# Last merge block finished by token thirds on VectorE, first output weights split one stage early, and constant products on TensorE ahead of the last stage

## What is computed

```
x = layer_norm(x_in)
z = x @ w_in + b_in                              # all projections and the merge gates
o_nsa, o_ml, o_fox = three token mixers of z     # 256 wide each
mix = (sum_b sigmoid(gate_b) * (o_b @ w_branch[b])) @ w_out
x1 = layer_norm(alpha * x + mix)
out = layer_norm(alpha * x1 + moe(x1))           # 16 experts, top group, then top 2 in it
```

## Time and profile before

| | us |
|---|---|
| three runs | 1513.5, 1512.06, 1507.91 |
| median of them | 1512.06 |
| profiled execution, its own time | 1509.91 |
| its span | 1508.3 |
| TensorE busy in it | 1368.0 (91%) |
| TensorE idle before the first product of mix (last product of merge to L2331) | 8.30 |
| TensorE idle before the last stage | 12.18 |

### The profile page before, as it was taken

One profiled execution on the slowest core, in us unless ns is written; L12 is line 12 of the kernel. 1 busy time (PEld: TensorE's weight loads), 2 busy tenths in 40 slices (PEclk: granted clock), 3 DMA queues, 4 the chain that ended last, 5 costly groups with the idle time before them and its releaser, 6 DMA issues. The chain is left out here.

```text
span 1508.3 us, 23664 instructions
## 1 busy us (share of the span) xinstructions
PE 1368.0 (91%) x8917; PEld 1185.3 (79%) x8917; DVE 611.7 (41%) x1593; ACT 516.6 (34%) x962; POOL 368.3 (24%) x463
## 2 busy tenths in 40 slices
PE   5999999999999999978888978979985999999965
PEld 3999999999888989956665657968865888888832
DVE  6222212222423324034667557863563233333317
ACT  5422222222122221126545656530001333434336
POOL 5211150020202000002333214621133322322307
PEclk9999999999999999969999999989995999999978
DMA  7244393162624224872004018762117787888954
GB/s 211 71 156 147 122 245 117 58 180 72 188 58 152 78 69 69 186 213 40 1 2 161 16 40 265 233 213 84 63 35 189 237 286 250 265 280 273 326 220 181
DMA packets 188963, 228.29 MB, mean 151 GB/s; under 512 B 47607, under 2 KB 157303, under 8 KB 187487
## 3 DMA queue, kind: packets, MB, share of 16 engines
q1 hardware_dynamic: 176270, 186.25, 41.1%
q0 software_dynamic: 12592, 40.71, 8.7%
HBM read 167.89 MB, written 60.19 MB: 151 GB/s over the span
## 5 line engine op out<-in xcount | busy, mean ns | idle before, releaser
L1255 PE MATMUL psum<-proj_x_hi,proj_w_hi 128*128 128x362 f32 (+1 forms) x1056 | 357.4, 338 | 3.4 <-DVE proj_w_lo L1380 2.2
L1255 PE MATMUL psum<-proj_x_hi,proj_w_lo 128*128 128x362 f32 (+1 forms) x1056 | 346.9, 329 | 0.0
L1255 PE MATMUL psum<-proj_x_lo,proj_w_hi 128*128 128x362 f32 (+1 forms) x1056 | 346.8, 328 | 0.0
L1255 PEld LDWEIGHTS psum<-proj_x_hi,proj_w_hi 128*128 128x128 f32 x1056 | 199.6, 189 | 10.4 <-POOL proj_x_lo L1461 2.5
L1255 PEld LDWEIGHTS psum<-proj_x_lo,proj_w_hi 128*128 128x128 f32 x1056 | 199.9, 189 | 0.0
L1255 PEld LDWEIGHTS psum<-proj_x_hi,proj_w_lo 128*128 128x128 f32 x1056 | 199.3, 189 | 0.0
L1380 DVE TENSOR_TENSOR proj_w_lo<-proj_w_raw,proj_w_hi 128x1024 fp32r<-128x1024 f32 x44 | 54.4, 1237 | 273.8 <-ACT proj_w_hi L1288 273.7
L1317 ACT ACTIVATE proj_sig<-psum,proj_bias 128x362 f32<-128x362 f32 (+1 forms) x72 | 40.4, 564 | 240.6 <-PE psum L1255 228.0
L2809 PEld LDWEIGHTS psum<-moe_xgt,expert_gate_w 128*128 128x128 f32 x512 | 85.2, 194 | 13.2 <-issue 13.2
L2809 PE MATMUL psum<-moe_xgt,expert_gate_w 128*128 128x192 f32 x512 | 92.1, 334 | 0.7 <-ACT moe_xgt L2854 0.7
L2809 PE MATMUL psum<-moe_xgt,expert_up_w 128*128 128x192 f32 x512 | 88.4, 326 | 0.0
(11 more groups left out here) (479 smaller groups left out, 2406.6 us busy)
## 6 DMA issues: line engine op xcount, KB each, us to landing
proj_w_raw<-in_w_in SPq DMA_DIRECT2D x43, 512.0 KB, 5.1
expert_gate_w<-in_moe_w_gate SPq DMA_DIRECT2D x16, 1024.0 KB, 5.6
expert_up_w<-in_moe_w_up SPq DMA_DIRECT2D x16, 1024.0 KB, 11.1
expert_down_w<-in_moe_w_down SPq DMA_DIRECT2D x16, 1024.0 KB, 8.0
merge_sig<-gate_scratch SPq DMA_DIRECT2D x24, 544.0 KB, 4.1
gate_scratch<-proj_sig SPq DMA_DIRECT2D x48, 181.0 KB, 2.0
feature_scratch<-proj_feat SPq DMA_DIRECT2D x13, 512.0 KB, 3.0
token_scratch<-proj_tok SPq DMA_DIRECT2D x10, 512.0 KB, 5.2
```

The lines of the kernel that those rows point to most:

```text
L1255: mm = nc.tensor.matmul(k.ps[u % RING][:, 0:w], b[wt][:, x % 2, kk, :], b[xx][:, kk, a0:a0 + w], start=(kk == 0 and i == 0), stop=(kk == K ...
```

## The change

1. In the last group of merge (g = 23) VectorE does the three adds itself, right after each third's multiplication, and POOL does none there. ScalarE makes `y_hi` of the last block in three copies, each after its third's add, and VectorE `y_lo` in three subtractions.
2. Piece 0 of `w_out` is split in merge: ScalarE's copy to `w0_hi` after its last sigmoid, VectorE's subtraction to `w0_lo` as the last of its list. Mix reads these for kk = 0 and splits only pieces 1 to 7; SP fetches piece 4 at once and pieces 5 to 7 after `w_lo` of pieces 1 to 3.
3. `XRES` falls from 4 to 2, so merge fetches two residual tiles, and mix fetches seven (two slots) where it fetched five.
4. After the experts TensorE multiplies the identity by 512 columns of constants 11 times into a PSUM bank that is not read (`keep_busy`), ahead of the last stage.

```diff
+def keep_busy(k, bank, n):
+    for _ in range(n):
+        k.nc.tensor.matmul(k.ps[bank][:, :], k.c("ident"), k.const[:, 0:512], start=True, stop=True)
...
-XRES = 4
+XRES = 2
...
+    pre |= {n: stack.enter_context(nc.sbuf_tensor(f"pre_{n}", [P, D], F32R)) for n in ("w0_hi", "w0_lo")}
...
@@ merge, scalar
-            high(KD - 1)
+                if g == UNITS - 1:
+                    act.wait_ge(ps["wo_loaded0"], 16)
+                    nc.scalar.copy(pre["w0_hi"][:, :], pre["w_raw"][:, 0, :]).then_inc(s["w0_hi_done"], 1)
+            for n, (a0, w) in enumerate(MCH):
+                act.wait_ge(s["ended"], n + 1)
+                nc.scalar.copy(y["hi"][:, KD - 1, a0:a0 + w], b["whole"][:, (KD - 1) % 2, a0:a0 + w]).then_inc(s["y_hi_done"], 1)
@@ merge, vector
-            low(KD - 1)
+                if g == UNITS - 1:
+                    dve.wait_ge(s["gated"], u + 1)
+                    dve.wait_ge(s["summed"], 6 * (KD - 1) + n + 1)
+                    nc.vector.tensor_tensor(dst, dst, b["part"][:, x % PARTS_AHEAD, 0:w], ALU.add).then_inc(s["ended"], 1)
+            for n, (a0, w) in enumerate(MCH):
+                dve.wait_ge(s["y_hi_done"], KD + n)
+                nc.vector.tensor_tensor(y["lo"][:, KD - 1, a0:a0 + w], b["whole"][:, (KD - 1) % 2, a0:a0 + w], y["hi"][:, KD - 1, a0:a0 + w].bitcast(F32), ALU.subtract).then_inc(s["y_lo_done"], 1)
+            dve.wait_ge(s["w0_hi_done"], 1)
+            nc.vector.tensor_tensor(pre["w0_lo"][:, :], pre["w_raw"][:, 0, :], pre["w0_hi"][:, :].bitcast(F32), ALU.subtract).then_inc(s["w0_lo_done"], 1)
@@ merge, gpsimd
-                if m:
+                if m and g < UNITS - 1:
@@ mix, sync
-                sp.wait_ge(s["w_lo_done"], kk - WRAW + 1)
+                if kk > WRAW:
+                    sp.wait_ge(s["w_lo_done"], kk - WRAW)
@@ mix, tensor
-                    if t == 0:
-                        pe.wait_ge(s["w_lo_done"], kk + 1)
+                    if t == 0 and kk >= 1:
+                        pe.wait_ge(s["w_lo_done"], kk)
...
+                            ws = b[ww][:, kk, :] if kk else pre["w0" + ww[1:]]
@@ mix, vector and scalar: the two loops that split the pieces
-            for kk in range(KD):
+            for kk in range(1, KD):
@@ experts, tensor
             all_rounds(pe, one_round)
+            keep_busy(k, 7, 11)
             last_tensor(pe)
```

More of the change, by code:

```diff
@@ L2063, in merge_branches @@
     st, b, s = phase(k, "merge", dict(sig=[P, SIGS, T], br_raw=[P, 3, 2, 364], br_hi=[P, 6, T], br_lo=[P, 6, T], branch_w=[P, RING, 2, P], branch_w_hi=[P, 2, 2, P], branch_w_lo=[P, 2, 2, P], part=[P, PARTS_AHEAD, 364], whole=[P, 2, T]),
-                     ["br_hi_done", "br_lo_done", "bw_hi_done", "bw_lo_done", "proj_mm", "sig_done", "gated", "summed", "y_hi_done", "y_lo_done"] + [f"br_loaded{m}_{n}" for m in range(3) for n in range(3)] + [f"sig_loaded{i}" for i in range(SIGS)] + [f"bw_loaded{i}" for i in range(RING)])
+                     ["br_hi_done", "br_lo_done", "bw_hi_done", "bw_lo_done", "proj_mm", "sig_done", "gated", "summed", "y_hi_done", "y_lo_done", "w0_hi_done", "w0_lo_done", "ended"] + [f"br_loaded{m}_{n}" for m in range(3) for n in range(3)] + [f"sig_loaded{i}" for i in range(SIGS)] + [f"bw_loaded{i}" for i in range(RING)])
     N = UNITS * 3
@@ L2281, in mix @@
                         for i, (yy, ww) in enumerate((("hi", "w_hi"), ("lo", "w_hi"), ("hi", "w_lo"))):
-                            mm = nc.tensor.matmul(k.ps[2 * (t % 2) + half][0:r, :], y[yy][:, kk, t * P:t * P + r], b[ww][:, kk, half * 512:(half + 1) * 512],
+                            ws = b[ww][:, kk, :] if kk else pre["w0" + ww[1:]]
+                            mm = nc.tensor.matmul(k.ps[2 * (t % 2) + half][0:r, :], y[yy][:, kk, t * P:t * P + r], ws[:, half * 512:(half + 1) * 512],
                                                   start=(kk == 0 and i == 0), stop=(kk == KD - 1 and i == 2))
@@ L2357, in low @@
             def low(kk):
-                dve.wait_ge(s["w_hi_done"], kk + 1)
+                dve.wait_ge(s["w_hi_done"], kk)
                 nc.vector.tensor_tensor(b["w_lo"][:, kk, :], pre["w_raw"][:, kk % WRAW, :], b["w_hi"][:, kk, :].bitcast(F32), ALU.subtract).then_inc(s["w_lo_done"], 1)
```

## The result

| | before | after |
|---|---|---|
| median of the runs of this comparison, us | 1506.72 (14) | 1500.4 (14) |
| lowest and highest run | 1501.55, 1513.5 | 1497.1, 1506.59 |
| ratio, 95% interval | | 0.9965 [0.9949, 0.9981] |
| span of the profiled execution | 1508.3 | 1501.0 |

The change makes the kernel faster by 0.35%, about 5.3 us (0.0035 x 1506.72). A second comparison gave 0.9971 [0.9953, 0.9989], 4.4 us. The forecast's shift, 4.6, lies between the two; its absolute time, 1506.4, is too high, and 1500.4 lies under the range's low end of 1501.5. Both have to be explained: the level, and what the right-looking sum is made of.

The account below looks back on a forecast made before the run. TensorE was taken to set the pace, with merge's end hanging on SP. Terms 3.5 + 0 + 0 + 1.1 = 4.6 us off a base of 1511.0 gave 1506.4, range 1501.5 to 1511.5.

Parts of the forecast that it names:

- the last of the sum: Whole kernel: the 4.6 us shift taken from a base of 1511.0, the middle of four known times, giving 1506.4.
- SP without two residual fetches: End of merge: SP ends 1.36 to 2.5 us earlier, middle 1.9, so mix's first instruction comes at 996.6.
- Rival (a): End of merge: VectorE or something else not SP holds the block; gain 2.7 at the least, 1508.3; chance 0.16.
- Adds on VectorE: Last group of merge: VectorE ends at 995.4 instead of 996.0, worth nothing by itself since SP ended later.
- The feared slowing of POOL: Last group of merge: POOL's adds meet VectorE's, third add 1.2 us later, VectorE ending at 996.6 as upper end.
- Piece 0 split ahead: Start of mix: the 1.56 us wait for the low part of the first weight piece goes wholly.
- merge to mix: From merge's last product to mix's first real one: that product comes at 997.4 instead of 1000.86, 3.5 us earlier.
- The clock at the start of mix: Start of mix: the clock falls again after a 6.4 us gap; no difference taken, -1.25 and +0.5 kept for the range.
- Two slots: Residual fetches in mix: tile t + 2 fetched in place of t + 4, 13.2 us of cover, cost nothing.
- rival (d): Residual add in mix, tiles 2 to 8: fetches are exposed and the kernel is slower, 1518.6; chance 0.03.
- Constant products: Before the last stage: eleven take 9.5 us, 2.7 stay idle, one low clock stretch; likeliest gain 1.1, ends 2.8 and -0.3.
- Rival (b): Gap before the last stage: no fall of the clock, total gain 6.3 us, 1504.7; chance 0.14.

Follow-up runs that it names:

- experiment 8: The unaltered changed kernel run twice more; 0.9971 beside the kernel before in one comparison, spans of its three traces 1501.0, 1495.5 and 1506.1.
- filler_only: The kernel before with only the eleven constant products added; ratio 0.998 [0.9963, 0.9997].
- six_pieces: The kernel before with VectorE's last y_lo of merge cut into six subtractions; one run, 1510.25 us.
- early_split_res_later: The changed kernel with piece 0 split at g = 21 and the residual tiles fetched in mix behind the pieces of w_out; ratio 0.9958 [0.9943, 0.9974].
- Experiments 2, 3, 5 and 6: In this order: two_slots_only; no_thirds; fetches_later and a sequel that also splits piece 0 at g = 21 (ratio 0.9954); early_split_res_later.
- experiment 4: The changed kernel with piece 0 of w_out split in mix as before; ratio 0.9971 [0.9957, 0.9985], merge to mix 7.72.
- two_slots_only: The kernel before with only XRES changed from 4 to 2; ratio 0.9989 [0.9974, 1.0004], merge to mix 8.45.
- no_thirds: The changed kernel with POOL's adds and whole y_hi and y_lo for the last block; ratio 0.9981 [0.9965, 0.9998], merge to mix 7.42.
- fetches_later: The changed kernel with seven small transfers moved from SP's merge list into mix, behind the pieces of w_out; ratio 0.9972 [0.9958, 0.9986].

## Why the prediction missed

**The level.** The step that failed is the last of the sum: "the four times known (with 1507.91 and 1513.5) have their middle at 1511.0, and from there it is 1506.4". The three runs shown (1507.91 to 1513.5) were high ones; the fourteen of the comparison have their median at 1506.72, 4.3 lower, and the four later groups of before lie at 1506.9 to 1508.5. With 1506.72 as the base the same shift of 4.6 gives 1502.1, inside the range; the remaining 1.7 is a shift of 6.3 by these two medians against the 4.6. The text counted 2 for the spread of medians, which was too little for a base of four executions: the fourteen runs of before spread over 12 (1501.55 to 1513.5), and experiment 8 shows traces of a single kernel 10.6 apart.

**SP without two residual fetches: undersized, by less than the first pair of traces says.** Forecast 1.9 (1.36 to 2.5). In the first pair SP came 3.63 earlier: 1.80 from issues where 1.36 stood, 1.50 from the standing of the two small fetches where about 0.5 was reckoned, and 0.27 from merge itself. Counted from merge's last product, SP ended after 7.62, 7.12 and 6.71 in the three traces with nothing of this part (before, filler_only, six_pieces), 7.15 in the mean, and after 4.26 to 5.01 in the eight traces with all of it, 4.75 in the mean. So the gain is 2.4, inside the stated 1.36 to 2.5.

The reason given, "3.96 for a fetch of four numbers per partition is no cost of its own: the queue was full", holds for a part only. The two small fetches (second router weights, first bias) stood together for 8.7 behind four residual tiles (three traces), 7.2 to 7.8 behind two (eleven traces), and still for 6.0 to 6.7 in the four kernels that had no residual tile just ahead of them. SP in early_split_res_later:

```profile
979.49 2.89 SPq L2103 DMA_DIRECT2D pre_w_r<-in_moe_w_expert  x1
982.42 3.47 SPq L2104 DMA_DIRECT2D pre_bias_r<-in_moe_b_group  x1
```

How much of these six is their own and how much comes from other transfers on the way is not separated by any run.

The reading that the block hung on SP was right for the kernel before (TensorE 0.68 after it). For the changed kernel SP at 995.9 and VectorE at 995.4 were forecast; they ended at 994.22 and 994.96 in the first trace, and level within 0.2 in the other seven. Not reckoned was that VectorE's end reaches TensorE sooner (0.32) than SP's (0.69), which keeps SP the holder in those seven. Rival (a), the block held by VectorE, came true in one trace of eight, by 0.37, and without its price: VectorE ended 1.6 before the feared 996.6. Experiments 2, 3, 5 and 6 show that VectorE is next as soon as SP's list is shortened or VectorE's lengthened.

**Adds on VectorE, "by itself this is worth nothing, since SP ended later": right by the rule, but needed in the sum.** The thirds were not run alone. With SP out of the way the arithmetic's end counts, and without the thirds the distance is 7.42. The feared slowing of POOL did not come: its first three adds of the block took 3.75, and the first three of the block ahead of it took 3.73 in the kernel before and 3.74 in the changed one, where nothing was moved; they ended at 990.06, before the forecast's 992. Of VectorE's adds only the first, which overlaps POOL's last, was a little longer (0.61 against 0.54).

**Piece 0 split ahead: right, a little undersized.** Forecast 1.56, experiment 4 shows 1.8. After the constants began, the real product came 0.42 later, not 0.77, so this way is 1.91 shorter (2.33 before). Waits for later pieces appear in three of the eight traces, 0.17 to 0.47 in all.

Together: merge to mix was forecast at 7.2 (997.4 - 990.23). Eight traces with the whole of this part have 5.74 to 6.12, mean 5.90; three without any of it 10.63, 10.14, 9.73, mean 10.17. The gain is 4.3 (2.4 and 1.9), forecast 3.5.

**The clock at the start of mix: near.** From the first product to the first residual add it is 13.64 in the mean of the same eight traces and 14.14 in that of the three: 0.5 gained where 0 was forecast, within what was kept open (from 1.25 gained to 0.5 lost).

**Two slots: right.** VectorE never waited for a residual fetch in mix; rival (d) had no part.

**Constant products: the mechanism right, the inference on the clock too firm.** 9.71 for 9.5, idle 2.34 for 2.7. "But 2.7 of idleness stay, and a gap of 1.97 was followed by a fall" rested on one gap of one trace. Over all traces the clock fell after that same 1.97 in 9 of 16, and after 2.3 to 2.6 behind eleven products in 3 of 11; after 5.00, 7.58 and 12 in 6 of 6. One low stretch after a short gap cost 1.1 to 1.7, about as forecast (1.7). So the first tile takes 3.96 in the mean of eleven traces with the products and 5.75 in the mean of four without (6.25, 5.30, 5.15, 6.31): they are worth 1.8, forecast 1.1. Rival (b) had too little chance at 0.14. The Trainium skill (TensorE: Matmul & The Clock Gate, Part 1) says that the monitor is free-running and that the slow matmuls at a kernel's start change in number from run to run of one kernel. The three traces of experiment 8 agree, at two places inside the kernel. The prediction quoted this rule for mix and did not apply it to the last gap or to the base.

**Not foreseen: 1.17 lost at the end of the last stage.** All thirteen traces with the thirds have a rest of 29.1, four without them 27.9 (before, filler_only, two_slots_only, no_thirds), and six_pieces 28.3. The meeting with POOL is shown; the pause that brings it about is not explained. The Trainium skill (GPSIMD Engine Reference, Specifications) has GpSimd and VectorE contend where VectorE reads two SBUF inputs; the trace agrees with 1.89 against 0.55 for VectorE's add beside POOL's. The prediction used that rule in merge, where the change was made, and not where the two engines also add side by side.

**The balance.** 4.3 + 0.5 + 1.8 - 1.2 = 5.4 by the means of the traces, 5.3 and 4.4 by the two comparisons. The forecast's 4.6 came out of three terms too small (merge to mix, clock in mix, last gap) and one loss left out. So the shift was near partly by luck, because these errors cancel, and the absolute time was off mainly by the base.

## What to carry over

Where a block ends on the slowest of several engines, write down the end of every engine's list: shortening the last list is worth only the distance to the next one, and an edit that is worth nothing alone (the thirds) pays once the first list is out of the way. Read who ends last from several traces, as here, where two engines are level. A gap that ends in low clock in one trace is one throw: look at the same gap in several executions before giving it a sign. Take the base from as many runs as there are, and widen for what one execution differs from another.

## What the runs showed of the hardware

- After a short gap the clock fell as TensorE took up work again, or a little later: in the third trace of the changed kernel it was 1.00 from 1454 to 1456, all idle, and 0.55 in the two us after, with the tile beginning at 1456.25. In the 12.18 of the kernel before it fell inside the gap: 0.62 from 1450 to 1452 and 0.50 from there to 1458, all idle. Gaps of 1.97 and 2.3 have either outcome in the same program.
- A pause of 0.25 or 0.26 on VectorE, with nothing to wait for, stood at one place of the last stage in four traces and one tile earlier in the thirteen whose list is longer by the thirds. There it cost 1.17 through a meeting with POOL.
- A block's end costs differently by who is last: 0.32 to 0.33 from VectorE's last instruction to TensorE's next, 0.68 to 0.69 from SP's last issue.
- SP stood 2.3 to 5.6 at the second router weights and 3.1 to 4.1 at the first bias in every kernel, wherever they were put: 2.78 and 3.33 even in fetches_later, where they are issued in mix.
